# The last nine token tiles of a decoder layer: half of the bank reads go from VectorE to ScalarE

## What is computed

```python
def _layer_norm(x, g, b):
    xf = x.astype(jnp.float32)
    mu = jnp.mean(xf, axis=-1, keepdims=True)
    var = jnp.mean(jnp.square(xf - mu), axis=-1, keepdims=True)
    return ((xf - mu) * lax.rsqrt(var + LN_EPS) * g.astype(jnp.float32) + b.astype(jnp.float32)).astype(x.dtype)

def _swiglu(x, w_gate, w_up, w_down):
    return (jax.nn.silu(x @ w_gate) * (x @ w_up)) @ w_down
...
    x = _layer_norm(DN_ALPHA * x + 0.5 * _swiglu(x, f2g, f2u, f2d), ln_g[2], ln_b[2])
```

## Time and profile before

| | us |
|---|---|
| median of the runs | 2025.29 (2023.71 to 2025.39) |
| the profiled execution | 2026.39 |
| its span | 2024.6 |
| TensorE, matmuls busy | 1962.7 (97%) |
| VectorE busy | 1066.7 (53%) |
| ScalarE busy | 664.1 (33%) |
| GpSimd busy | 937.9 (46%) |
| first matmul of the last nine tiles, from the span's start | 1982.42 |
| last matmul of the program starts | 2010.12 |
| last store is issued | 2021.52 |

### The profile page before, as it was taken

The page is one execution under the profiler, slowest core; times in us unless marked ns, Lnnn a source line. Parts: engine busy times, 40 slices in busy tenths (PEclk is TensorE's granted clock), DMA queues, the critical chain, the costliest instruction groups (busy, mean ns, idle before and its releaser), DMA issues. The chain is left out here.

```text
span 2024.6 us, 29594 instructions
## 1 busy us (share of the span) xinstructions
PE 1962.7 (97%) x11245; PEld 1798.6 (89%) x11245; DVE 1066.7 (53%) x1687; ACT 664.1 (33%) x996; POOL 937.9 (46%) x459
## 2 busy tenths in 40 slices
PE   7999999999999999999999999999999999999997
PEld 7999999999788879999797567899999999978885
DVE  7444444444877871001565635744444444487787
ACT  5222222222432252111145544422232232243324
POOL 4654665554543432221453423556456656444423
PEclk9999999999999999999999999999999999999998
DMA  4334434337855322111124012233443443685532
GB/s 164 127 129 174 150 126 172 133 126 238 319 181 175 125 81 71 42 41 31 38 80 162 20 42 109 79 127 126 144 182 126 145 160 126 219 318 190 170 119 88
DMA packets 101069, 272.27 MB, mean 134 GB/s; under 512 B 17919, under 2 KB 22527, under 8 KB 95615
## 3 DMA queue, kind: packets, MB, share of 16 engines
q1 hardware_dynamic: 100991, 271.21, 38.9%
HBM read 188.34 MB, written 82.84 MB: 134 GB/s over the span
## 5 line engine op out<-in xcount | busy, mean ns | idle before, releaser
L701 POOL TENSOR_TENSOR f_w_low<-f_w_raw,f_w_hi 128x1024 fp32r<-128x1024 f32 x86 | 211.5, 2460 | 393.9 <-DVE f_s_raw L969 392.1
L799 PE MATMUL bank<-x_hi,f_w_hi 128*128 128x320 f32 (+1 forms) x1008 | 321.8, 319 | 1.2 <-ACT f_part L579 1.2
L800 PE MATMUL bank<-x_low,f_w_hi 128*128 128x320 f32 (+1 forms) x1008 | 321.8, 319 | 0.0
L801 PE MATMUL bank<-x_hi,f_w_low 128*128 128x320 f32 (+1 forms) x1008 | 321.4, 319 | 0.0
L707 POOL TENSOR_TENSOR f_s_low<-f_s_raw,f_s_hi 128x1024 fp32r<-128x1024 f32 x84 | 218.7, 2604 | 0.0
L799 PEld LDWEIGHTS bank<-x_hi,f_w_hi 128*128 128x128 f32 x1008 | 189.8, 188 | 1.8 <-ACT f_part L579 1.8
L800 PEld LDWEIGHTS bank<-x_low,f_w_hi 128*128 128x128 f32 x1008 | 189.8, 188 | 0.0
L801 PEld LDWEIGHTS bank<-x_hi,f_w_low 128*128 128x128 f32 x1008 | 189.7, 188 | 0.0
L767 POOL TENSOR_TENSOR f_T_low<-f_T_raw,f_hi_T 128x1024 fp32r<-128x1024 f32 x40 | 102.9, 2574 | 139.4 <-ACT f_hi_T L579 139.4
L1070 DVE TENSOR_TENSOR acc<-acc,bank 128x512 f32<-128x512 f32 x184 | 117.7, 680 | 37.3 <-PE bank L916 27.9
L1007 DVE TENSOR_TENSOR f_part<-bank,f_part 128x384 f32<-128x384 f32 x42 | 23.4, 558 | 208.8 <-PE bank L801 208.8
(11 more groups left out here) (324 smaller groups left out, 4845.5 us busy)
## 6 DMA issues: line engine op xcount, KB each, us to landing
f_w_raw<-ffn_in SPq DMA_DIRECT2D x86, 512.0 KB, 5.0
h_rows<-f_h_full SPq DMA_DIRECT2D x44, 544.0 KB, 6.1
h_sums_rows<-f_h_sums SPq DMA_DIRECT2D x20, 1056.0 KB, 9.0
f_d_sums<-ffn_in SPq DMA_DIRECT2D x20, 1024.0 KB, 7.9
d_sums_rows<-f_d_sums SPq DMA_DIRECT2D x20, 1024.0 KB, 6.5
f_S_raw<-h_sums_rows SPq DMA_DIRECT2D x40, 512.0 KB, 3.8
f_T_raw<-d_sums_rows SPq DMA_DIRECT2D x40, 512.0 KB, 4.9
f_A_raw<-h_rows SPq DMA_DIRECT2D x30, 512.0 KB, 3.8
```

Of the source, the lines that this page charges most:

```text
L701: pool.tensor_tensor(flat(b_.w_lo[s][j]), flat(raw), flat(b_.w_hi[s][j]).bitcast(F32), SUB)\
L799: pe.matmul(out, hi[k], x_hi[k], start=first and k == 0, stop=False, skip_group_check=not first)
L800: pe.matmul(out, hi[k], x_lo[k], start=False, stop=False, skip_group_check=not first)
L801: mm = pe.matmul(out, lo[k], x_hi[k], start=False, stop=k == last, skip_group_check=not first)
```

## The change

In the block that ends the program (`ends` is true where `norm.y_out` is set), the odd positions 1, 3, 5 and 7 are read by ScalarE. For these, TensorE adds the tile's row of `acc` into the bank by one more matmul with `norm.ident`, a 128x128 float identity. ScalarE then copies each bank into `acc` and sums it along the way (`read_row`), ahead of that position's `deviation`, and counts in a semaphore of its own, `rows_read`. VectorE keeps the even positions, and its `mean` at odd ones waits for ScalarE. `row_read(n)` names the semaphore and the count that tell that half n was read.

```diff
+    ends = norm.y_out is not None
+
+    def scalar_reads(p):
+
+        return ends and p % 2 == 1
+
+    def row_read(n):
+
+        p, half = n // 2, n % 2
+        if scalar_reads(p):
+            return norm.past(norm.rows_read, 2 * (p // 2) + half + 1)
+        return past(down_free, LAST_FROM + (2 * (p // 2) + half if ends else n) + 1)
...
+        if ends:
+            for p in range(TOKEN_TILES):
+                if scalar_reads(p):
+                    read_row(act, p)
+                norm.deviation(act, p)
+            return
...
-            pe.wait_ge(*past(*((down_free, LAST_FROM + n - 3) if n > 3 else read_of(ROUNDS - 1, "P4", n) if n < 3
-                               else read_of(ROUNDS - 1, "D1"))))
+            if n > 3:
+                pe.wait_ge(*row_read(n - 4))
+            else:
+                pe.wait_ge(*past(*(read_of(ROUNDS - 1, "P4", n) if n < 3 else read_of(ROUNDS - 1, "D1"))))
+            if n == 2 and scalar_reads(p):
+                pe.wait_ge(*past(*read_of(ROUNDS - 1, "D1")))
...
-                mm = pe.matmul(out[:, :], high, w_l, start=False, stop=g == 1)
+                mm = pe.matmul(out[:, :], high, w_l, start=False, stop=g == 1 and not scalar_reads(p))
+            if scalar_reads(p):
+                mm = pe.matmul(out[:, :], norm.ident[:, :], acc[:, t, d], start=False, stop=True)
             mm.then_inc(down_done, 1)
+
+    def read_row(act, p):
+
+        for half in range(2):
+            n, d = 2 * p + half, slice(HALF * half, HALF * half + HALF)
+            act.wait_ge(*past(down_done, LAST_FROM + n + 1))
+            act.activation(acc[:, ORDER[p], d], core.banks[4 + n % 4][:, :], ACT.Copy, accum_out=norm.row_sum(p, half))\
+               .then_inc(norm.rows_read, 1)
...
-        for half in range(2):
+        for half in () if scalar_reads(p) else range(2):
             n, d = 2 * p + half, slice(HALF * half, HALF * half + HALF)
             dve.wait_ge(*past(down_done, LAST_FROM + n + 1))
-            dve.wait_ge(*past(down_free, LAST_FROM + n))
+            semaphore, value = row_read(n)
+            dve.wait_ge(semaphore, value - 1)
...
-        norm.mean(dve, p, past(down_free, LAST_FROM + 2 * p + 2))
+        norm.mean(dve, p, row_read(2 * p + 1))
...
+        self.rows_read = self.hi_done
```

## The result

| | before | changed |
|---|---|---|
| median of 15 runs | 2024.13 us (2020.31 to 2026.96) | 2027.80 us (2024.88 to 2030.77) |
| ratio of the runs | | 1.0018, 95% from 1.0011 to 1.0025 |
| profiled execution: its time / its span | 2026.39 / 2024.6 us | 2028.75 / 2026.9 us |
| from VectorE's last read of the round ahead to the end of the span | 41.91 us | 45.12 us |

The changed kernel is 3.7 us slower by the medians (the interval: 2.2 to 5.1 us). Whether the loss is over 0.2% these runs don't settle; that it isn't zero they do.

The account below looks back on a forecast made before the run. It took the start of position 7's deviation on ScalarE, set by TensorE's queue with eight identity matmuls at 1.23 us, as the bound: 6.1 us later, so 2025.29 + 6.1 = 2031.4 us, range 2028.6 to 2033.0.

Parts of the forecast that it names:

- the price of the identity: On TensorE, each of eight identity matmuls at odd positions was to add 1.23 us to its half (1.00 to 1.33).
- TensorE's sum: From position 0's end at 1985.33: 14 halves 19.04, two `fold`s 2.46, eight identities 9.84 us; position 7 done at 2016.67.
- the square: Start of position 7's deviation on ScalarE, forecast at 2017.72 against 2011.59, 6.1 us later.
- the cheap case: Rival: cheap identity, ScalarE's queue the bound, 2026.0 to 2028.1 us; also middle prices with TensorE the bound; chance 0.11.
- One number carries the forecast: When ScalarE can begin position 7's deviation sets the end: `gain` 2.50 us later, then 8.17 us to the end.
- VectorE's 6.3 us: Eight bank reads of 0.79 us taken off VectorE at odd positions; credited nothing, to become a wait there.
- The rival of VectorE's surplus: VectorE was the bound and the reads its surplus: 6.3 us off the end, 2019.0 us, faster; chance 0.04.
- No wait of TensorE on its new readers: TensorE would not wait for banks read by ScalarE; position 3 has 2.2 us to spare, later ones more.
- The rival of a late ScalarE: Position 1's reads over 2.2 us later than put, so TensorE waits at position 3: 2033 us and up; chance 0.05.
- The `shift` of position 6 held by GpSimd: Sign: on VectorE this `shift` waits for GpSimd's `gain` of position 7, which runs until 2022.6.
- The middle case: Identity at 0.91 us, four ordinary matmuls, TensorE still the bound: 2028.9 us; counted within the cheap case.
- term for ScalarE's reads: Each of eight bank reads with a sum on ScalarE at odd positions takes 0.72 us (0.60 to 0.84).

Follow-up runs that it names:

- e2: Changed kernel with the 128-column identity matmul moved behind each odd half's first matmul; ratio to the kernel before 1.0016.
- e1: Changed kernel with the identity matmul cut to 64 columns and moved behind each odd half's first matmul; ratio to the kernel before 1.0028.
- e4: Changed kernel with the identity matmuls kept but the odd positions' bank reads given back to VectorE; ratio to the kernel before 1.0012.
- e3: Changed kernel without the identity matmuls (row not added at odd positions), ScalarE still reading those banks; ratio to the kernel before 1.0011.
- e8: Changed kernel with the decode tile's `fold` constant widened by zeros from 64 to 128 columns; ratio to the kernel before 1.0016.
- e9: Kernel before, with a small square root ahead of position 0's deviation to load ScalarE's table early; ratio to the kernel before 1.0008.

## Why the prediction was half right

**What failed: the price of the identity, in TensorE's sum.** The prediction took 1.23 us from `fold`, the nearest row, with 1.00 and 1.33 as ends, though `fold` has 64 output rows and the identity 128. That difference is the one that mattered: 128 columns cost 0.89 (changed kernel and e2), 64 cost 1.22 to 1.23 (`fold`, and e1 at the same place). The true price lay below both ends of the bound. The prediction had named its own sign for this: odd halves under 2.3 us apart; they are 2.25. Eight times 0.34 are 2.7 us too much; the square was forecast 6.13 later and came 3.28 later, 2.85 less. Of the remaining 0.13, the last read gives 0.05: from its start to the square are 0.97 us (2012.99 to 2013.96) where the sum had 0.72 + 0.05 + 0.25 = 1.02. The rest lies ahead of that read, on TensorE's path.

The text had the better number beside it. The Trainium skill (FP8 and Floating Point Precision, TensorE Precision Notes) counts four passes for true FP32, and with 0.227 us a pass that makes an estimate of 0.91. The trace after agrees for 128 columns, with 0.89, and not for the 64 of `fold`. I wrote that the trace disagreed, and let one row of another width outweigh it. With 0.91 the text's own figure was +3.6 us, against +3.7 by the medians and 3.28 for the square.

**A smaller miss: the base.** The forecast stood on 2025.29, the median of three runs of the kernel before. Fifteen runs put it at 2024.13, 1.16 lower. Of the 3.6 us between 2031.4 and 2027.80 the base is 1.2 and the size 2.4. As a difference the range began at 3.3 us (2028.6 - 2025.29), and the measured 3.7 lies in it, but only in the part that the range took over from the cheap case: the sum's own bounds, +4.2 to +7.0, miss it.

**What held, with the size of one term changed:**

- *One number carries the forecast.* The square moved by 3.28 and the stretch by 3.21; in nine runs the two never part by over 0.1 us. The `gain` follows 2.50 us later, as in the earlier trace rows, and the tail of 8.17 is 8.10.
- *The sum itself.* e1 has the price that was forecast and comes out at +6.23 against +6.1. Price times eight on TensorE's path, nothing hidden by another engine, was the right mechanism at that price.
- *VectorE's 6.3 us bring nothing.* They became a wait for ScalarE (12.5 us in four pieces), and in e4, where VectorE keeps all its reads, the time is the same. The rival of VectorE's surplus is refuted: VectorE was busy for 95% of a window, and taking work off it moved the end the wrong way by e3's 2.33 us, before any identity. The Trainium skill (Perfetto Trace Analysis, Optimizing Scalar/DVE Operations) says that moving work to ScalarE may make sense where VectorE is saturated; here it did not.
- *No wait of TensorE on its new readers.* None in the changed kernel. The rival of a late ScalarE did not happen there; in e3, with TensorE 7.1 us faster, it shows with 1.1 us.
- *The `shift` of position 6 held by GpSimd.* It starts at 2017.22 and ends 1.09 us behind the `gain`.

**What was closer than it seemed.** The rival with a cheap identity and ScalarE's queue as the bound put ScalarE's floor at +0.7 to +2.8; e3 measures +2.33. It was to decide from a price of 0.97 down, and 0.89 is below that. But 0.97 is where the sum falls to the 4.05 us that count as none (6.13 - 2.08), and not where ScalarE's queue passes TensorE; by the squares of the changed kernel and e3 (3.28 and 2.33) that lies near 0.77, an estimate (0.89 - 0.95 / 8). The middle case that the text put there, TensorE still the bound with a cheaper matmul, is what happened. The prediction gave that whole case 0.11, since it took `fold` as nearly certain. Its term for ScalarE's reads was too high in a row: 0.57 from read to read (2003.91 to 2004.48 at position 5, by the same timeline) against 0.72, as the read of the sum lies beside the reads. The 0.22 in that term was taken behind a square whose follower waits for it (`n1_squared`); the second of two reads has no such wait.

## What to carry to other kernels

Price an added operation by a row that agrees in every dimension of the tile, and if there is none, don't take the nearest one as a lower bound: look at what its weight loads wait for, since a narrower matmul can be the dearer one. When work moves from a busy engine to an idle one, ask what it will stand behind in the new engine's queue: ScalarE had idle time, and its eight reads still cost 2.33 us. And when a change has two halves, time each alone: here both delay the same event, and undoing either would have bought at most 0.9 us.

## What the runs showed of the hardware that was not expected

- A plain-float matmul of 128x512 adds 0.89 us to a half with 128 columns of weights and 1.22 to 1.23 with 64. With 128 the weights load while the matmuls ahead run; with 64 the load starts with the matmul (idle 0.35 to 0.56 ahead of it, 0.81 behind), and the next matmul takes 0.43 in the chain instead of 0.23. Filling the other 64 columns with zeros saved 0.34 us per matmul (e8). Why the narrow load isn't taken ahead no row shows.
- ScalarE's reads of a bank with a sum follow each other at 0.57 us, though the row of one is 0.58 and the read of its sum another 0.19: the latter begins 0.1 us before the read ends and adds nothing to the step. Behind a 1024-wide square the next instruction starts 0.22 us behind the start of that read the earlier trace rows, but it also waits for the square.
- GpSimd's `gain`s step by 3.3 and 4.3 us in turn in the later positions, in the kernel before and in e9. A `shift` of 1.28 us when alone took 3.20 when it began 0.29 us behind a `gain`. In e9 an earlier start came out as the other order of the two, and not as an earlier end.
